# A mixture-of-experts stage with gate/up cut in halves around two transposes, gathers and weight splits moved ahead (Trainium2, one core)

## What is computed

```python
hidden = (silu(einsum('nd,edf->nef', hf, w_exp_gate)) * einsum('nd,edf->nef', hf, w_exp_up))
y = einsum('nef,efd->nd', hidden * combine[..., None], w_exp_down)
```

## Time and profile before

| | |
|---|---|
| median of three runs | 1435.9 us (1431.64 to 1437.26) |
| profiled execution | 1432.76 us |
| its span | 1431.0 us |
| TensorE matmul busy, share of the span | 1125.9 us, 79% |
| VectorE busy | 802.8 us, 56% |
| ScalarE busy | 644.6 us, 45% |
| GpSimd busy | 480.8 us, 34% |
| first token turn of the expert stage | at 1002.06 us |

### The profile page before, as it was taken

How to read it: one execution, slowest core, us unless ns; L and a number is a source line. 1 busy time by engine, 2 the same in 40 slices (tenths; PEclk the granted TensorE clock), 3 DMA queues, 4 the chain that set the end, 5 groups by cost and what they waited for, 6 DMA issues and landing times. The chain is left out here.

```text
span 1431.0 us, 19400 instructions
## 1 busy us (share of the span) xinstructions
PE 1125.9 (79%) x5872; PEld 937.6 (66%) x5872; DVE 802.8 (56%) x1183; ACT 644.6 (45%) x1048; POOL 480.8 (34%) x313
## 2 busy tenths in 40 slices
PE   3378999997999497989986698873899999999800
PEld 0256777775988386888885577753677777777600
DVE  0444454313554476677773455525668777787367
ACT  0323111113322374566664455511777777688412
POOL 0000000003000366366772122220566665776341
PEclk8588999998999799899998799985899999999955
DMA  6541757713100442453312322203887897743275
GB/s 243 180 144 52 283 178 244 232 59 91 40 8 0 119 103 71 111 122 84 83 31 61 134 90 97 92 30 104 280 293 240 292 329 253 263 134 101 89 257 183
DMA packets 121726, 207.51 MB, mean 145 GB/s; under 512 B 13128, under 2 KB 83816, under 8 KB 119614
## 3 DMA queue, kind: packets, MB, share of 16 engines
q1 hardware_dynamic: 113196, 177.01, 37.7%
q0 software_dynamic: 7344, 26.74, 5.8%
q10 hardware_dynamic: 1122, 2.95, 0.6%
HBM read 218.27 MB, written 45.02 MB: 184 GB/s over the span
## 5 line engine op out<-in xcount | busy, mean ns | idle before, releaser
L88 POOL TENSOR_TENSOR moe_wd_lo<-moe_wd,moe_wd_hi 128x1024 fp32r<-128x1024 f32 x66 | 163.9, 2504 | 102.0 <-ACT moe_wd_hi L2041 102.0
L88 DVE TENSOR_TENSOR moe_wgu_lo<-moe_wgu,moe_wgu_hi 128x1024 fp32r<-128x1024 f32 x132 | 174.2, 1379 | 41.3 <-ACT moe_wgu_hi L2035 41.2
L2035 ACT CAST moe_wgu_hi<-moe_wgu 128x1024 fp32r x132 | 128.7, 1051 | 66.5 <-DMA moe_wgu<-in_w_exp_up 66.3
L93 PE MATMUL proj_acc_ps<-proj_w_hi,hidden_hT_hi 128*128 128x512 f32 x288 | 120.0, 417 | 2.4 <-DVE hidden_hT_lo L88 2.4
L94 PE MATMUL proj_acc_ps<-proj_w_lo,hidden_hT_hi 128*128 128x512 f32 x288 | 115.5, 401 | 0.0
L95 PE MATMUL proj_acc_ps<-proj_w_hi,hidden_hT_lo 128*128 128x512 f32 x288 | 115.4, 401 | 0.0
L1250 POOL TENSOR_TENSOR att_e<-att_e 128x1152 f32<-128x1152 f32 (+1 forms) x36 | 86.0, 2389 | 74.0 <-DVE att_e L1317 74.0
L93 PE MATMUL moe_gu_ps<-moe_wgu_hi,moe_xT_hi 128*128 128x512 f32 x264 | 106.2, 402 | 4.7 <-DVE moe_xT_lo L88 4.7
L623 POOL MEMSET conv_ones<- 128x128 f32 x1 | 0.2, 204 | 325.6 <-POOLq L83 325.6
L94 PE MATMUL moe_gu_ps<-moe_wgu_lo,moe_xT_hi 128*128 128x512 f32 x264 | 105.7, 401 | 0.0
L95 PE MATMUL moe_gu_ps<-moe_wgu_hi,moe_xT_lo 128*128 128x512 f32 x264 | 105.6, 400 | 0.0
(11 more groups left out here) (333 smaller groups left out, 2744.9 us busy)
## 6 DMA issues: line engine op xcount, KB each, us to landing
moe_wgu<-in_w_exp_gate SPq DMA_DIRECT2D x34, 1024.0 KB
moe_wgu<-in_w_exp_up SPq DMA_DIRECT2D x34, 1024.0 KB
moe_wd<-in_w_exp_down SPq DMA_DIRECT2D x34, 1024.0 KB
scratch_y_slots<-moe_y SPq DMA_DIRECT2D x33, 512.0 KB, 3.6
ada_w<-in_w_ada SPq DMA_DIRECT2D x8, 1024.0 KB, 11.6
proj_raw<-in_w_in SPq DMA_DIRECT2D x32, 256.0 KB, 6.4
proj_mods<-in_w_ada SPq DMA_DIRECT2D x4, 2048.0 KB, 8.7
proj_xh<-in_w_ada SPq DMA_DIRECT2D x4, 2048.0 KB, 9.3
```

The lines of the kernel that those rows point to most:

```text
L88: return eng.tensor_tensor(low, value, high.bitcast(F32), ALU.subtract)
L93: pe.matmul(out, a_high, b_high, start=start, stop=False)
L2035: act.copy(wgu_hi[:, k.buf, j:j + 2], wgu[:, buf, j:j + 2]).then_inc(gu_hi_done, 1)
```

## The change

New orders of the bodies, block t:

- TensorE: first half of gate/up of t+1, turn hidden of t, turn tokens of t+2, second half of gate/up of t+1, down of t.
- ScalarE: high part of the tokens of t+2 in two halves, silu of t+1, two pieces of gate/up of t+3, copy y of t, the other two pieces, high part of down of t+2.
- VectorE: both parts of the turned hidden of t, last piece of gate/up of t+2, tokens of t+2 in two halves, hidden of t+1, first three pieces of gate/up of t+3.
- GpSimd: gather of t+3, low part of down of t+2.

The token halves have their own semaphores, and the first half of the high part of t+2 waits only for the first half of gate/up of t+1 (`gu_half_done`). SyncE's program and all buffers stay as they are. The diff, cut to its core:

```diff
@@ gpsimd
             def body(t, left):
+                if left >= 3:
+                    gather(t.next().next().next())
                 if left >= 2:
-                    gather(t.next().next())
-                buf = weight_buffer(pool, t)
-                pool.wait_ge(d_hi_done, t.n + 1)
+                    d_low(t.next().next())
+
+            def d_low(k):
+                buf = weight_buffer(pool, k)
+                pool.wait_ge(d_hi_done, k.n + 1)
                 for half in range(2):
-                    op = split_low(pool, wd_lo[:, t.buf, half], wd[:, buf, half], wd_hi[:, t.buf, half])
+                    op = split_low(pool, wd_lo[:, k.buf, half], wd[:, buf, half], wd_hi[:, k.buf, half])
                 op.then_inc(d_lo_done, 1)
+
             gather(Step(0, 0))
             gather(Step(0, 1))
+            gather(Step(0, 2))
+            d_low(Step(0, 0))
+            d_low(Step(0, 1))
             blocks(pool, body)
@@ tensor
+            def gate_up(k, half):
+                pe.wait_ge(x_lo_done[half], k.n + 2)
+                if half == 0:
+                    pe.wait_ge(gu_lo_done, k.n + 3)
+                    pe.wait_ge(hid_done, k.n + 1)
+                for j in range(half * (KT // 2), (half + 1) * (KT // 2)):
...
+                mm.then_inc(gu_done if half else gu_half_done, 1)
+
+            def body(t, left):
+                if left >= 1:
+                    gate_up(t.next(), 0)
+                turn_hidden(t)
                 if left >= 2:
                     turn_x(t.next().next())
+                if left >= 1:
+                    gate_up(t.next(), 1)
                 pe.wait_ge(hidT_done, t.n + 2)
...
             turn_x(Step(0, 0))
-            gate_up(Step(0, 0))
+            gate_up(Step(0, 0), 0)
             turn_x(Step(0, 1))
+            gate_up(Step(0, 0), 1)
@@ scalar
-            def x_high(k):
+            def x_high(k, half):
                 act.wait_ge(x_turned, k.n + 3)
-                act.wait_ge(gu_done, k.n + 2)
-                act.copy(xT_hi[:], x_ps[:]).then_inc(x_hi_done, 1)
+                if half == 0:
+                    act.wait_ge(gu_half_done, k.n + 1)
+                else:
+                    act.wait_ge(gu_done, k.n + 2)
+                cols = slice(half * 512, (half + 1) * 512)
+                act.copy(xT_hi[:, cols], x_ps[:, cols]).then_inc(x_hi_done[half], 1)
...
             def body(t, left):
                 if left >= 2:
-                    gu_high(t.next().next())
-                if not (isinstance(t.n, int) and t.n == 0):
-                    evacuate(Step(t.i, t.c - 1))
+                    x_high(t.next().next(), 0)
+                    x_high(t.next().next(), 1)
                 if left >= 1:
-                    d_high(t.next())
                     silu(t.next())
+                if left >= 3:
+                    ahead = t.next().next().next()
+                    buf = weight_buffer(act, ahead)
+                    gu_high(ahead, buf, range(0, KT // 2, 2))
+                evacuate(t)
+                if left >= 3:
+                    gu_high(ahead, buf, range(KT // 2, KT, 2))
                 if left >= 2:
-                    x_high(t.next().next())
...
+                    d_high(t.next().next())
...
@@ vector
             def x_low(k):
-                dve.wait_ge(x_hi_done, k.n + 1)
-                split_low(dve, xT_lo[:], x_ps[:], xT_hi[:]).then_inc(x_lo_done, 1)
+                for half in range(2):
+                    cols = slice(half * 512, (half + 1) * 512)
+                    dve.wait_ge(x_hi_done[half], k.n + 1)
+                    split_low(dve, xT_lo[:, cols], x_ps[:, cols], xT_hi[:, cols]).then_inc(x_lo_done[half], 1)
...
             def body(t, left):
-                hidden(t)
-                if left >= 2:
-                    gu_low(t.next().next())
                 dve.wait_ge(h_turned, t.n + 3)
...
                 if left >= 2:
+                    gu_low(t.next().next(), range(KT - 2, KT, 2))
                     x_low(t.next().next())
...
+                if left >= 1:
+                    hidden(t.next())
+                if left >= 3:
+                    gu_low(t.next().next().next(), range(0, KT - 2, 2))
```

More of the change, by code:

```diff
@@ L1891, in expert_stage @@
         gu_hi_done, gu_lo_done, d_hi_done, d_lo_done = (s.sem(k) for k in ("gu_hi_done", "gu_lo_done", "d_hi_done", "d_lo_done"))
-        idx_done, started, x_turned, x_hi_done, x_lo_done = (s.sem(k) for k in ("idx_done", "started", "x_turned", "x_hi_done", "x_lo_done"))
+        idx_done, started, x_turned = (s.sem(k) for k in ("idx_done", "started", "x_turned"))
+        x_hi_done, x_lo_done = ([s.sem(f"{k}{half}") for half in range(2)] for k in ("x_hi_done", "x_lo_done"))
+        gu_half_done = s.sem("gu_half_done")
         gu_done, silu_done, hid_done, h_turned = (s.sem(k) for k in ("gu_done", "silu_done", "hid_done", "h_turned"))
@@ L1980, in _ @@
             pe.sem_inc(gu_done, 2)
+            pe.sem_inc(gu_half_done, 1)
             pe.sem_inc(h_turned, 2)
@@ L1984, in turn_x @@
                 pe.wait_ge(xg_in[k.buf], k.nth * 16 + 16)
-                pe.wait_ge(x_lo_done, k.n + 1)
+                pe.wait_ge(x_lo_done[1], k.n + 1)
                 for j in range(KT):
@@ L1988, in turn_x, with turn_hidden @@
                 mm.then_inc(x_turned, 1)
[L1990 to L2002, removed]
+            def turn_hidden(t):
                 pe.wait_ge(hid_done, t.n + 3)
@@ L2028, in _, with gu_high @@
             act.sem_inc(y_out, 16)
[L2030 to L2034, removed]
+            def gu_high(k, buf, pieces):
+                if pieces[0] == 0:
+                    act.wait_ge(gu_in[k.buf], k.nth * 32 + 32)
+                    act.wait_ge(gu_done, k.n + 1)
+                for j in pieces:
                     act.copy(wgu_hi[:, k.buf, j:j + 2], wgu[:, buf, j:j + 2]).then_inc(gu_hi_done, 1)
@@ L2059, in body @@
                 if left >= 2:
-                    gu_high(t.next().next())
-                if not (isinstance(t.n, int) and t.n == 0):
-                    evacuate(Step(t.i, t.c - 1))
+                    x_high(t.next().next(), 0)
+                    x_high(t.next().next(), 1)
                 if left >= 1:
-                    d_high(t.next())
                     silu(t.next())
-                if left >= 2:
-                    x_high(t.next().next())
-            gu_high(Step(0, 0))
-            x_high(Step(0, 0))
-            gu_high(Step(0, 1))
+                if left >= 3:
[5 more added lines that the diff above has]
+                    gu_high(ahead, buf, range(KT // 2, KT, 2))
+                if left >= 2:
+                    d_high(t.next().next())
+            gu_high(Step(0, 0), weight_buffer(act, Step(0, 0)), range(0, KT, 2))
+            x_high(Step(0, 0), 0)
+            x_high(Step(0, 0), 1)
+            gu_high(Step(0, 1), weight_buffer(act, Step(0, 1)), range(0, KT, 2))
+            x_high(Step(0, 1), 0)
+            x_high(Step(0, 1), 1)
+            silu(Step(0, 0))
             d_high(Step(0, 0))
-            silu(Step(0, 0))
-            x_high(Step(0, 1))
+            gu_high(Step(0, 2), weight_buffer(act, Step(0, 2)), range(0, KT, 2))
+            d_high(Step(0, 1))
             blocks(act, body)
-            evacuate(Step(0, BLOCKS - 1))
         @block.vector
@@ L2080, in _, with gu_low @@
             dve.sem_inc(gu_lo_done, 2)
-            dve.sem_inc(x_lo_done, 1)
+            for half in range(2):
+                dve.sem_inc(x_lo_done[half], 1)
             dve.sem_inc(hid_done, 2)
             dve.sem_inc(hidT_done, 1)
-            def gu_low(k):
+            def gu_low(k, pieces):
                 buf = weight_buffer(dve, k)
-                for j in range(0, KT, 2):
+                for j in pieces:
                     dve.wait_ge(gu_hi_done, k.n * (KT // 2) + (j // 2 + 1))
                     op = split_low(dve, wgu_lo[:, k.buf, j:j + 2], wgu[:, buf, j:j + 2], wgu_hi[:, k.buf, j:j + 2])
-                op.then_inc(gu_lo_done, 1)
+                if pieces[-1] == KT - 2:
+                    op.then_inc(gu_lo_done, 1)
             def x_low(k):
-                dve.wait_ge(x_hi_done, k.n + 1)
-                split_low(dve, xT_lo[:], x_ps[:], xT_hi[:]).then_inc(x_lo_done, 1)
+                for half in range(2):
+                    cols = slice(half * 512, (half + 1) * 512)
+                    dve.wait_ge(x_hi_done[half], k.n + 1)
+                    split_low(dve, xT_lo[:, cols], x_ps[:, cols], xT_hi[:, cols]).then_inc(x_lo_done[half], 1)
             def hidden(k):
@@ L2111, in body @@
                 if left >= 2:
+                    gu_low(t.next().next(), range(KT - 2, KT, 2))
                     x_low(t.next().next())
-            gu_low(Step(0, 0))
+                if left >= 1:
+                    hidden(t.next())
+                if left >= 3:
+                    gu_low(t.next().next().next(), range(0, KT - 2, 2))
+            gu_low(Step(0, 0), range(0, KT, 2))
```

(4 more changed lines are left out.)

3 lines of the change are left out of this document (added).

## The result

The changed kernel takes 1523.0 us (median of 4 runs, 1518.6 to 1530.5) against 1435.7 for the kernel before on the same chip (median of 4): a ratio of 1.061, 95% interval 1.059 to 1.064, **87 us slower**. The profiled execution took 1518.6, with a span of 1516.9 against 1431.0.

A forecast was written before the change was run, and what follows sets the result against it. Expert stage taken as close to TensorE's work, 9.55 us a block; late gathers make 30 steps 375.3 against 311.4 us: +63.9, less 3.4, 1.3 and 0.7, +58.5. That gave 1494 us on the median, range 1447 to 1525.

The forecast's parts named there:

- The likeliest case: Expert stage: TensorE's token turn waits for a late gather and the clock falls; +58.5 us, 1494 us, chance 0.45.
- the prediction's mark R: On TensorE, R(t) is the moment gate/up of block t+1 ends and releases ScalarE; R(0) to R(30) put at 375.3 us.
- pairs of "22 to 26": Sign in the expert stage: two blocks take 22 to 26 us, also in the last ten, without weight loads.
- GpSimd's share: Chain to the gather's issue: GpSimd's two low halves of down 4.75 us, index copy and wait 0.95.
- the worse rival: GpSimd's index copy takes 1.19 us, not 0.18, and gathers land in 8.3 and 5.6: +101, 1537 us, chance 0.08.
- The clock: TensorE's clock falls after the gather wait, slowing turn and half gate/up: 1.7 us a pair, bounds 0 and 3.4.
- L: Landing time of GpSimd's gather: taken as 6.0 us beside weight loads and 4.9 after them.
- The landing "as if alone" of a rival: Gathers land in 4.2 us despite weight loads, with a full clock: +11, 1447 us, chance 0.08.
- a gain of 3.4: Start of the expert stage: 2.36 us gap before 1017.39 plus an estimated 1.0 of wait before the first gate/up.
- the clock did not hold: Rival: the gather is late but TensorE's clock holds; pairs 23.65 and 22.55 us, +33, 1469 us, chance 0.30.
- in time: Rival: GpSimd's gather is in time, landing 3.95 us before gate/up's end: -28, 1408 us, chance 0.07.
- The ring of 19.3 for faster pairs: Loads and stores through SyncE: y copied earlier takes out 1.95 us, 19.3 a pair while weights load.

The follow-up runs named there:

- Experiment 8: The changed kernel with VectorE making one of four low gate/up pieces, which TensorE reads for all eight slices: 1507.3 us, ratio 1.050.
- experiment 3: The changed kernel with 20 matmuls whose result is not used ahead of the token turn in odd blocks: 1500.1 us, ratio 1.046.
- experiment 2: The changed kernel with the gather put between GpSimd's two halves of down's low part: 1508.0 us, ratio 1.052.
- experiment 1: The changed kernel, but GpSimd makes the low part of down of t+1, not t+2, behind the gather of t+3: 1438.0 us, ratio 1.002.
- experiment 4: The kernel before, with only ScalarE's copy of y moved between the second and third of its four gate/up pieces: 1422.6 us, ratio 0.991.
- experiment 6: Experiment 1 with all four low gate/up pieces of t+3 together at the end of VectorE's body: 1419.6 us, ratio 0.988.

## Why the prediction was right, and where its sizes were not

The likeliest case came true, with its mechanism: TensorE waits in this stage on gathered tokens, and the index copy follows directly on the low part. The range held it only just (1523 of 1447 to 1525; one of the four runs, at 1530, lies above it), and the forecast was 1494. Against the kernel before I put +58.5, and it is +87. The 30 steps were put at 375.3 and took 406, 31 more. From the prediction's mark R, the end of gate/up, the start gained 5.3 (put 3.4, and 1.1 of it comes from before the stage) and the end 2.8 (put 2.0). Of the signs, pairs of "22 to 26" were 25.2 to 27.4, and one wait on the turned hidden was there after all, the 8.3 of the first step. Term by term:

- **GpSimd's share.** I took the low part at 4.75, near the shortest of before, and 0.95 from its end to the issue. Measured 5.56 and 1.94 (1216.82 to 1218.76): +1.8 a pair. VectorE's pieces of the next gate/up run at that time. I had seen the copy of 1.19 and put it into the worse rival as bad luck; about half of the copies before were that long, and in this order all are that a waited-for gather stands behind. Experiment 8 shows the cause for the copy; the low part stayed at 5.2 and more there, so its excess is only partly explained.
- **The clock.** Put at 1.7 a pair. In all 15 blocks with a wait of 3.4 us or more behind the start, the turn took 1.97, and from its start to down's first matmul it took 5.1 to 6.5 us, with no wait between, in place of the 3.7 of the other blocks: 2.1 on average, 32 us in all. The trace agrees with the gap of before, and experiment 3 shows that it costs time.
- **The landing.** L = 6.0 was right in size from block 10 on (5.8 to 6.2), and 4.9 for the pairs without loads a little high (4.4 to 4.7). But as a constant it was wrong: most of it is what remains of the gate load, which is why experiment 8 gained nothing there, and experiment 2 next to nothing. From block 10 on there is a second chain that I did not price: gate load, 11.1 to the turn, 5.9 to the end of gate/up (1230.7), 4.2 for half copy, silu, two pieces and y to the store at 1234.94, and 6.15 over SyncE's down load to the next gate load at 1241.09: 27.4. GpSimd's chain, 7.75 + 0.2 + 5.56 + 1.94 + 6.1 + 5.9, gives 27.4 as well. So a shorter low part or copy alone gains nothing there (experiment 8).
- **The four pairs behind the first** took 25.7 on average against 25.35, which looks right and is luck. Their waited-for gathers did not go out beside a gate load but 19 to 20 us behind one, and landed in 4.4 to 4.7:

```profile
1060.99 1.10 POOL L1962 DMA_INDIRECT moe_xg<-scratch_h,moe_idx  x1 [0.84 <-POOL moe_idx L1959]
...
1065.73 1.97 PE L1998 MATMUL moe_x_ps<-all_ident,moe_xg 128*128 128x128 f32 x8 [4.49 <-DMA moe_xg<-scratch_h,moe_idx]
```

  L was 1.4 too long there, and GpSimd's 1.8 too short made up for it. The landing "as if alone" of a rival came true in these pairs.
- Together: pairs with loads 27.4 in place of 25.35 from block 10 on, pairs without 25.2 to 26.4 in place of 24.25. That makes +13 and +6, and the four pairs +1.5.
- **The first pair.** 35.6 in place of 25.35: +10, the largest single miss. I had costed the moved work at the start as a gain of 3.4. The first hidden turn did come earlier, but then:

```profile
1016.85 12.28 POOL L88 TENSOR_TENSOR moe_wd_lo<-moe_wd,moe_wd_hi 128x1024 fp32r<-128x1024 f32 x4 [11.46 <-ACT moe_wd_hi L2059]
1017.82 9.10 DVE L88 TENSOR_TENSOR moe_wgu_lo<-moe_wgu,moe_wgu_hi 128x1024 fp32r<-128x1024 f32 x3 [2.44 <-ACT moe_wgu_hi L2053]
1027.33 0.43 DVE L88 TENSOR_TENSOR moe_hidT_lo<-moe_h_ps,moe_hidT_hi 128x256 fp32r<-128x256 f32 x1
1027.81 0.79 PE L93 MATMUL moe_y_ps<-moe_wd_hi,moe_hidT_hi 128*128 128x512 f32 x1 [8.26 <-DVE moe_hidT_lo L88]
```

  These are rows of the kernel after. VectorE's three pieces for block 2, now ahead of the loop, take 9.10 in place of 3.6, GpSimd's four halves 12.28 in place of some 9.6. The hidden's copy is queued behind VectorE's, and TensorE stands 8.26 us. But that wait is not what the pair costs: in experiment 8, without these pieces, the first step takes 11.9 and TensorE then stands for the gather of block 3, so that the pair is only 2.6 shorter. Its rows there, gather and turn:

```profile
1027.94 0.98 POOL L1962 DMA_INDIRECT moe_xg<-scratch_h,moe_idx  x1 [0.82 <-POOL moe_idx L1959]
...
1036.60 1.97 PE L1998 MATMUL moe_x_ps<-all_ident,moe_xg 128*128 128x128 f32 x8 [9.16 <-DMA moe_xg<-scratch_h,moe_idx]
```

  In front of that gather GpSimd now makes the low parts of two blocks, four halves, some 9.6 us even undisturbed, where the sum had one block's. I looked at what the start gained and not at what now stands in front of the first turned hidden and of the first gather of the loop.

One slip of the prediction changes nothing: the gather issued at 1188.26 is that of block 19, not 20.

Of the Trainium skill I had weighed one rule, DMA: Bandwidth & Descriptors, section Queues, rings and completion order: engines go round their queues packet by packet. By that a gather issued 1.3 us earlier beside the same load should be read earlier. The runs do not agree: in experiment 8 it was read 11.3 behind the gate load, in the changed kernel 11.1. Only a start right behind the load helped, and by less than its head start.

Another of its pages speaks of the meeting of VectorE and GpSimd. The Trainium skill, GPSIMD Engine Reference, sections Specifications and Key points, says that GpSimd shares its SBUF interfaces with VectorE and contends with VectorE instructions that have two SBUF inputs. The traces agree: the long rows above are such subtractions on both sides (5.43 in place of 1.2 us, 12.28 in place of 9.6).

The other rivals: the clock did not hold, and "in time" fell with experiment 1, which shows that it needs the other order. The ring of 19.3 for faster pairs was not contradicted: experiments 4 and 6 reach steps of 9.9 and 9.5 to 9.7 beside most loads.

**Open.** Why a gather lands so late beside a load (which queue or engine holds it back), and why experiment 2's land late without one, was not tried. Nor was a version that keeps experiment 6 and shortens its first step by an earlier load or a shorter queue on GpSimd. The rows put the half clock at 32 us of TensorE's time and the filler won back 23; the rest is not separated.

## What to carry to other kernels

Before a transfer is moved "ahead", read what stands in front of it on its engine: here the gather of t+3 was written in an earlier body and yet issued later, because the split put before it waits for the last thing in another engine's body. Price that chain from end to end, and its reader with it, since both moved towards each other. When a change has several parts, try each alone: moving one copy of 1 us (experiment 4) brought 12 us, while the whole lies 100 above it.

## What the runs showed of the hardware that I had not expected

- Two subtractions with both inputs in SBUF, one on VectorE and one on GpSimd, do not run side by side at full speed but hold each other: 1.2 us became 5.43 on VectorE, begun 0.4 behind 4.73 of GpSimd (experiment 1), and a copy of 128 numbers on GpSimd took 1.18 in place of 0.18 behind a VectorE piece.
- A gather of 128 rows issued 1.7, 3.7 or 5.0 us behind the first of a block's weight loads was read 10.9, 11.3 and 11.1 us behind it; issued 0.5 behind, others were read at 7.9 to 10.1. With no gate load in the 19 us before it, it landed in 4.4 to 4.7 in the changed kernel.
- The clock was at half after each of the 15 waits of 3.4 to 6.3 us on a gather inside the steps of the changed kernel (turn 1.97 us), and not after those of 0.36 and 0.54 (1.09). It came back within the same block (0.50 from 1224.84 to 1228.20, 1.00 from 1230.70). Matmuls without use in the wait made the kernel 23 us faster.
